# Front of a decoder step: squares of x in column strips, u in chunk order, all splits of x first, every low part on DVE

## Chip, cores and metric

One core of a Trainium2 chip runs one launch of the kernel. The metric is the time of that launch on the device in microseconds, median of several runs.

## What is computed

One inference step of a decoder layer, for a prompt of 512 tokens and eight samples of one token each. The kernel holds them together as T = 520 columns, with the 1024 features on the partitions (8 tiles of 128). The reference, cut to the part that the change touches:

```python
h = _rmsnorm(x, lp['g_mix'])                       # x * rsqrt(mean(x*x) + eps) * g
proj = h @ lp['w_in']                              # 1024 -> 2048
q, k, v, u = jnp.split(proj, [512, 1024, 1536], axis=-1)
...
lam_bar = jnp.exp(lam * dt)                        # S5: 32 groups, 64 complex states each
b_bar = ((lam_bar - 1.0) / lam)[..., None] * bmat
bu = jnp.einsum('gnp,btgp->btgn', b_bar, ug)
_, hs = lax.associative_scan(combine, (decay, bu), axis=1)     # h[t] = lam_bar*h[t-1] + bu[t]
y = jnp.einsum('gpn,btgn->btgp', cmat, hs).real + d_skip * ug
```

Behind it come stick-breaking attention over q, k, v (for the samples with paged keys and values), a gated output of the state-space part, the output projection, cross-attention into 256 memory tokens, a gated MLP with a convolution, and a final norm.

## The kernel before

Five engines run instruction lists of their own and meet at semaphores. The order on each is written out by hand.

**Weights.** All weights pass as 126 blocks of 128x1024 floats. SP loads block n into one of four raw buffers, once the low part of block n-4 is there. ACT rounds it to `w_hi` (`high(n)`, L1292), and a second engine subtracts to get `w_lo` (`low(n)`): DVE for the blocks in `DVE_LOWS` (whole, L1656), POOL for the others (two halves, L589). Both buffers are double. `high(n)` waits until block n-2 has been multiplied.

**A projection** (`project`, L625 to L627) takes 8 tiles of x, two halves of 260 columns, and three matmuls each (hi*hi, hi*lo, lo*hi): 48 matmuls. Blocks 0 to 3 give u, 4 to 7 q, 8 to 11 k, 12 to 15 v. Results stand in two alternating PSUM slots; DVE reads them, times the inverse root of the mean square `rinv` (`read_inputs`, L1769; `project_read`, L1809 and L1812), and a block waits for the read of the one two before it.

**Start.** ACT takes x in eight tiles: it rounds x*g to `h_hi` (L1311), DVE subtracts for `h_lo` (L1648), and ACT squares the tile into one of two buffers (L1325). TensorE multiplies block 0 tile by tile and after each tile adds the squares of that tile over the partitions, with a stationary of ones (128 wide, two matmuls of 260 columns in plain fp32, L707). ACT then takes the root (Ln, Exp, L1302 and L1303). Between the splits DVE computes powers of lambda on 128x16 operands.

**State-space part.** The prompt is cut into 128 chunks of 4 tokens. `turn_channels` (L719) brings u from (channel, time) into 32-row strips by position in the chunk: 64 matmuls with a slice of the identity, whose moving operand is every fourth column of u. `turn_weights` (L729) transposes the weights built by `lag_weights`, `lag_kernel` (L751) multiplies them with C, in 32 matmuls that fill 32-row strips, ACT copies the results (L1372, L1384). `chunk_states` (L770) gives the input of each chunk's state; DVE rotates it by the chunk's angle, scans over the chunks and rotates back (`rotate`, `scan`, `turn_back`, L1847 to L1873). The chunk angles are made on 128x2048 operands: ACT scales (L1347), DVE rounds off the whole turns (L1817 to L1819) and makes the absolute value (L1821), ACT takes two Sins (L1378, L1379). These steps lie between the projections of q and k. Then the first attention scores follow (L918), capped by DVE (L1933).

## Time and profile before

| | |
|---|---|
| median of 3 runs | 878.95 us (876.35 to 880.17) |
| profiled execution, own time | 880.04 us |
| its span | 878.3 us |
| TensorE matmul busy | 847.1 us (96%) |
| TensorE weight loads busy (beside the matmuls) | 797.1 us (91%) |
| DVE busy | 465.6 us (53%) |
| ACT busy | 334.0 us (38%) |
| POOL busy | 270.9 us (31%) |
| granted TensorE clock, mean | 0.991 of full |

Busy time is averaged over stages with different limits; in the first sixth of the span DVE is busy nearly all the time, later half of it. The page of the profile cuts the span in 40 slices of 22 us: DVE has 5, 9, 6, 9, 9, 8 tenths in the first six, TensorE 5, then 9 in nearly all. The chain that ended last is 84% TensorE.

### The profile page before, as it was taken

Reading aid. Unit: us, or ns where it says so; the run is one execution under the profiler, and the core shown is the slowest. Engines: PE = TensorE matmul, PEld = TensorE weight load, DVE = VectorE, ACT = ScalarE, POOL = GpSimd, SP = SyncE. Lnnn points to the kernel's source line nnn. Section 1 sums busy time; section 2 is a strip of 40 time slices with the busy share of each in tenths; the row PEclk is TensorE's granted clock in tenths of the full one; section 3 lists DMA queues with packets and bytes.
Section 4 is the critical chain, followed back from the end, with each engine's and each line's share of the span. In section 5 each row is a group of like instructions: output and inputs, shape, how many; then the busy total and the mean of one; then the engine's idle time right before and its main releaser. Section 6 shows DMA issues by size and latency. Waiting matters only on the chain.

```text
span 878.3 us, 17246 instructions
## 1 busy us (share of the span) xinstructions
PE 847.1 (96%) x7422; PEld 797.1 (91%) x7422; DVE 465.6 (53%) x674; ACT 334.0 (38%) x491; POOL 270.9 (31%) x213
## 2 busy tenths in 40 slices
PE   5999999999999999998999999999999999999996
PEld 4989998877888999995599999999999999999995
DVE  5969998777337735112323665656555666011013
ACT  6534415554745425113322633333333334222221
POOL 4100002010360151440025244444444444445560
PEclk9999999998999999999999999999999999999998
DMA  8211213233654485218412223322233322333312
GB/s 324 75 50 49 74 49 150 100 86 109 189 162 154 144 322 230 96 50 321 206 48 88 83 96 97 97 91 84 91 97 96 97 84 88 99 102 112 96 54 97
DMA packets 30459, 103.99 MB, mean 118 GB/s; under 512 B 3866, under 2 KB 6170, under 8 KB 27954
## 3 DMA queue, kind: packets, MB, share of 16 engines
q1 hardware_dynamic: 30386, 102.91, 34.8%
q8 instruction: 58, 0.95, 0.5%
q14 instruction: 15, 0.12, 0.0%
HBM read 96.28 MB, written 6.71 MB: 117 GB/s over the span
## 4 chain that ended last, share of the span: by engine, by line
PE 84%; DVE 5%; DMA 4%; ACT 4%; SPq 1%; issue 1%; POOL 0%; DVEq 0%; ACTq 0%
PE pj L625 22%; PE pj L627 22%; PE pj L626 22%; DMA w_raw<-in 3%; PE pj L1221 2%; PE aux L1152 2%; PE pj L632 2%; PE pj L634 1%; PE pj L633 1%; PE pj L918 1%; PE aux L707 1%; PE aux L719 1%; DVE near L1933 1%; PE aux L918 1%; ACT near L1424 1%
## 5 line engine op out<-in xcount | busy, mean ns | idle before, releaser
L589 POOL TENSOR_TENSOR w_lo<-w_raw,w_hi 128x512 fp32r<-128x512 f32 x196 | 260.6, 1350 | 553.9 <-ACT w_hi L1292 553.8
L625 PE MATMUL pj<-h_hi,w_hi 128*128 128x260 f32 x1312 | 374.4, 285 | 12.2 <-POOL w_lo L589 10.8
L627 PE MATMUL pj<-h_hi,w_lo 128*128 128x260 f32 x1312 | 371.3, 283 | 0.0
L626 PE MATMUL pj<-h_lo,w_hi 128*128 128x260 f32 x1312 | 370.1, 282 | 0.0
L625 PEld LDWEIGHTS pj<-h_hi,w_hi 128*128 128x128 f32 x1312 | 247.5, 189 | 14.1 <-POOL w_lo L589 10.8
L1292 ACT ACTIVATE w_hi<-w_raw 128x1024 fp32r<-128x1024 f32 x125 | 132.1, 1057 | 311.4 <-PE pj L627 274.0
L626 PEld LDWEIGHTS pj<-h_lo,w_hi 128*128 128x128 f32 x1312 | 247.3, 188 | 0.4
L627 PEld LDWEIGHTS pj<-h_hi,w_lo 128*128 128x128 f32 x1312 | 247.4, 189 | 0.0
L627 PE MATMUL pj<-a_hi,w_lo 128*128 128x260 f32 x336 | 95.0, 283 | 0.0
L625 PE MATMUL pj<-a_hi,w_hi 128*128 128x260 f32 x336 | 94.9, 282 | 0.0
L626 PE MATMUL pj<-a_lo,w_hi 128*128 128x260 f32 x336 | 94.9, 282 | 0.0
L627 PEld LDWEIGHTS pj<-a_hi,w_lo 128*128 128x128 f32 x336 | 63.3, 189 | 0.0
L625 PEld LDWEIGHTS pj<-a_hi,w_hi 128*128 128x128 f32 x336 | 63.2, 188 | 0.0
L626 PEld LDWEIGHTS pj<-a_lo,w_hi 128*128 128x128 f32 x336 | 63.2, 188 | 0.0
L2175 DVE TENSOR_TENSOR x<-pj,x 128x520 f32<-128x520 f32 x7 | 4.9, 700 | 88.4 <-PE pj L627 88.4
L2171 DVE TENSOR_TENSOR a_lo<-conv,a_hi 128x520 f32 x22 | 38.2, 1736 | 18.3 <-ACT a_hi L1614 18.3
L1644 DVE TENSOR_TENSOR acc<-acc,sq 128x520 f32<-128x520 f32 (+1 forms) x29 | 31.5, 1087 | 25.5 <-ACT sq L1298 25.5
L1611 ACT ACTIVATE conv<-conv 128x520 f32<-128x520 f32 x22 | 14.1, 639 | 74.6 <-DVE conv L2164 74.6
L1656 DVE TENSOR_TENSOR w_lo<-w_raw,w_hi 128x1024 fp32r<-128x1024 f32 x27 | 33.0, 1222 | 14.5 <-ACT w_hi L1292 14.3
L2160 DVE SCALAR_TENSOR_TENSOR conv<-gate,cols,conv 128x512 f32<-128x512 f32 x22 | 39.6, 1799 | 0.0
L2074 DVE TENSOR_TENSOR x<-pj,x 128x520 f32<-128x520 f32 x16 | 11.2, 699 | 35.4 <-PE pj L627 35.4
L2156 DVE TENSOR_TENSOR gate<-pj,rinv 128x520 f32<-128x520 f32 x22 | 15.4, 700 | 26.8 <-PE pj L627 26.5
(374 smaller groups left out, 1205.1 us busy)
## 6 DMA issues: line engine op xcount, KB each, us to landing
w_raw<-in SPq DMA_DIRECT2D x126, 512.0 KB, 3.5
caches<-in SPq DMA_DIRECT2D x14, 1024.0 KB, 12.3
vpg<-in SPq DMA_DIRECT2D x16, 256.0 KB, 2.9
kpg<-in SPq DMA_DIRECT2D x12, 256.0 KB, 3.0
x<-in SPq DMA_DIRECT2D x4, 520.0 KB, 8.4
out<-x SPq DMA_DIRECT2D x16, 130.0 KB, 1.9
out<-kT SPq DMA_DIRECT2D x1, 1040.0 KB
far<-in SPq DMA_DIRECT2D x1, 1024.0 KB, 4.8
```

The lines of the kernel that those rows point to most:

```text
L589: nc.gpsimd.tensor_tensor(lo[:, part], w_raw[:, n % 4, part], hi[:, part].bitcast(F32), ALU.subtract).then_inc(lo_done, 1)
L625: pe.matmul(out, s_hi, m_hi_, start=first, stop=False)
L626: pe.matmul(out, s_hi, m_lo_, start=False, stop=False)
L627: ins = pe.matmul(out, s_lo, m_hi_, start=False, stop=last)
L632: pe.matmul(out, stationary[0], moving[0], start=first, stop=False, skip_group_check=True)
L918: pe.matmul(at(h, i, P * i), kT[r0:r0 + DH, pair, P * i:P * (i + 1)], qT[r0:r0 + DH, pair, P * i:TP], start=(i < 3), stop=False, skip_grou ...
L1152: ins = pe.matmul(aux[:, 2 * (h % 2) + qt // 2, MT * (qt % 2):MT * (qt % 2 + 1)], qm[:, 2 * h + dd, P * qt:P * (qt + 1)], mkT[:, 2 * h + d ...
L1292: nc.scalar.activation(w_pair(n)[0], w_raw[:, n % 4, :], ACT.Copy).then_inc(hi_done, 1)
L1644: tt(acc[:, 0:width], acc[:, 0:width], sq[:, 0:width], ALU.add).then_inc(acc_added, 1)
L1656: tt(w_lo[:, n % 2, :], w_raw[:, n % 4, :], w_hi[:, n % 2, :].bitcast(F32), ALU.subtract).then_inc(dve_lo, 1)
L2160: order.done(stt(out=conv[:, c, 0:TP], in0=gate[:, c, 1:TP + 1], scalar=tap("conv_w1"), in1=conv[:, c, 0:TP], op0=ALU.mult, op1=ALU.add))
L2171: tt(a_lo[:, i * 2 + c, :], conv[:, c, :], a_hi[:, i * 2 + c, :].bitcast(F32), ALU.subtract).then_inc(a_split, 1)
```

## The change

- Squares: each of the eight tiles gets a buffer of its own (in tiles that are written later), so squares need no wait. TensorE sums them behind two tiles of block 1: four strips of 130 columns, each into 32 output rows, then ACT copies the strips to SBUF, and four matmuls with 32 contracted rows spread the sums to 128 rows (hence the factor GP in the mean).
- Splits: ACT rounds tiles 1 to 7 with only square 0, the angles and `high(1)` between; the other squares follow. DVE makes all low parts of x before the powers. SP loads x ahead of blocks 2 and 3 and the constants.
- Low parts 0, 1 and 2 go from POOL to DVE.
- u: `read_inputs` writes u by position in the chunk, so that `turn_channels` and the copies of the samples' u read it accordingly.
- Chunk angles: one rounding, and one fused operation (rounded minus ROUND minus angle, so the sign is turned); the absolute value goes to ACT.
- Order: `lag_kernel` goes ahead of the turned weights, its copy on ACT ahead of theirs; `input_products` and `input_weights` go behind the read of block 1 and low part 3; each of `read_inputs` 2 and 3 goes ahead of the lag weights beside it; `turn_back(0)` and low part 10 shift by one place; high(4) waits for the chunk numbers. POOL's two semaphores of the padding become one.

```diff
-DVE_LOWS = tuple(range(3, 16)) + tuple(range(N_MV, N_OUT + 2)) + (N_MQ, N_MQ + 1, N_GU, N_GU + 1)
+DVE_LOWS = tuple(range(16)) + tuple(range(N_MV, N_OUT + 2)) + (N_MQ, N_MQ + 1, N_GU, N_GU + 1)
...
+        def square_of_x(kt):
+            return (acc[:, :], sq[:, :], kT[:, 2, :], qT[:, 0, :], qT[:, 1, :], qT[:, 2, :], qT[:, 3, :],
+                    kT[:, 3, :])[kt]
+
+        QUARTER = T // 4
+
...
-            for c in range(4):
+            def load_x(c):
                 eng.dma_start(x[:, 2 * c:2 * c + 2, :], xT[:, 2 * c:2 * c + 2, :]).then_inc(x_loaded[c], 16)
-                load_block(c)
-                if c == 0:
-                    eng.dma_start(consts[:, :, :], consts_d).then_inc(consts_loaded, 16)
+
+            load_x(0)
+            load_block(0)
+            load_x(1)
+            load_block(1)
+            load_x(2)
+            load_x(3)
+            eng.dma_start(consts[:, :, :], consts_d).then_inc(consts_loaded, 16)
+            load_block(2)
+            load_block(3)
             eng.dma_start(bmat, bc_d[:, 0:2]).then_inc(s5_loaded, 16)
             eng.dma_start(cmat, bc_d[:, 2:4]).then_inc(s5_loaded, 16)
...
-            low(0)
-            low(1)
             pool.wait_ge(consts_loaded, 16)
             nc.gpsimd.tensor_copy(consts_r[:, :, :], consts[:, 0:3, :]).then_inc(consts_rounded, 1)
-            low(2)
-            pool.wait_ge(x_summed, KT)
+            pool.wait_ge(x_summed, 1)
             nc.gpsimd.memset(u_last, 0.0).then_inc(u_zeroed, 1)
             low(16)
             low(17)
             pool.wait_ge(y_done, 5)
...
                               halves(h_lo[:, kt, :])[:, a, :]) for a in range(2)], kt == 0, kt == KT - 1)
-                if kt == KT - 1:
-                    ins.then_inc(block_done, 1)
-                if kt == 0:
-                    pe.wait_ge(consts_loaded, 16)
-                pe.wait_ge(x_squared, kt + 1)
-                for a in range(2):
-                    ins = pe.matmul(aux[:, a, 0:HALF], ones, halves((sq, acc)[kt % 2][:, :])[:, a, :],
-                                    start=(kt == 0), stop=(kt == KT - 1))
+            ins.then_inc(block_done, 1)
+
+            def sum_squares():
+
+                pe.wait_ge(consts_loaded, 16)
+                for kt in range(KT):
+                    pe.wait_ge(x_squared, kt + 1)
+                    for s in range(4):
+                        ins = pe.matmul(aux[GP * s:GP * (s + 1), 3, 0:QUARTER], ones[:, 0:GP],
+                                        square_of_x(kt)[:, QUARTER * s:QUARTER * (s + 1)],
+                                        start=(kt == 0), stop=(kt == KT - 1), skip_group_check=True)
                 ins.then_inc(x_summed, 1)
+
+            def spread_sums():
+
+                pe.wait_ge(x_copied, 1)
+                for s in range(4):
+                    ins = pe.matmul(aux[:, s, 0:QUARTER], ones[GP * s:GP * (s + 1), :],
+                                    rinv[GP * s:GP * (s + 1), 0:QUARTER], start=True, stop=True,
+                                    skip_group_check=True)
+                ins.then_inc(x_summed, 1)
+
             def turn_channels():
 
                 pe.wait_ge(evacuated, 4)
...
-                        moving = uT[:, a, 0:TP].rearrange("p (c j) -> p j c", j=CH)
+                        moving = uT[:, a, :].rearrange("p (j c) -> p j c", j=CH)[:, :, 0:NCH]
...
             def turn_weights(g):
                 b, wt = g // 2, (wtre, wtim)[g % 2]
+                if g == 2:
+                    pe.wait_ge(kernel_copied, 1)
+                if g == 3:
+                    pe.wait_ge(rc_copied, 1)
                 if g >= 4:
                     pe.wait_ge(w2_copied, g - 1)
                 for r in range(4):
...
             def lag_kernel():
 
-                pe.wait_ge(w2_copied, 8)
+                pe.wait_ge(wt_built, 1)
...
             def turn_kernel():
 
-                pe.wait_ge(kernel_copied, 1)
+                pe.wait_ge(w2_copied, 8)
...
 
-            for n in range(1, N_Q + 1):
+            ready(1, 1)
+            for kt in range(KT):
+                if kt == 2:
+                    sum_squares()
+                if kt == KT // 2:
+                    second_half(1)
+                if kt == KT // 2:
+                    spread_sums()
+                hi, lo = weight(1, kt)
+                ins = three([(slot(1)[:, a, :], hi, lo, halves(h_hi[:, kt, :])[:, a, :],
+                              halves(h_lo[:, kt, :])[:, a, :]) for a in range(2)], kt == 0, kt == KT - 1)
+            ins.then_inc(block_done, 1)
+            for n in range(2, N_Q + 1):
                 project(n, n)
             turn_channels()
             project(N_Q + 1, N_Q + 1)
             column_scales()
-            pe.wait_ge(wt_built, 1)
-            for g in range(3):
+            lag_kernel()
+            for g in range(4):
                 turn_weights(g)
-            pe.wait_ge(rc_copied, 1)
-            turn_weights(3)
             project(N_Q + 2, N_Q + 2)
             chunk_states(0)
             for g in range(4, 8):
...
             def square_x(kt):
-                if kt >= 2:
-                    act.wait_ge(x_summed, kt - 1)
-                nc.scalar.activation((sq, acc)[kt % 2][:, :], x[:, kt, :], ACT.Square).then_inc(x_squared, 1)
-
-            for kt in range(KT):
+                nc.scalar.activation(square_of_x(kt), x[:, kt, :], ACT.Square).then_inc(x_squared, 1)
+
+            def split_x(kt):
                 act.wait_ge(x_loaded[kt // 2], 16)
                 split_high(kt, "g_mix")
-                if kt == 0:
-                    high(0)
-                if kt == 2:
-                    high(1)
+
+            split_x(0)
+            high(0)
+            split_x(1)
+            square_x(0)
+            act.wait_ge(angle_done, 1)
+            nc.scalar.activation(sm[:, 11, :], sm[:, 9, :], ACT.Exp)
+            nc.scalar.activation(sm[:, 14:16, :], sm[:, 12:14, :], ACT.Sin).then_inc(polar_done, 1)
+            split_x(2)
+            split_x(3)
+            high(1)
+            for kt in range(4, KT):
+                split_x(kt)
+            for kt in range(1, KT):
                 square_x(kt)
-                if kt == 1:
-                    act.wait_ge(angle_done, 1)
-                    nc.scalar.activation(sm[:, 11, :], sm[:, 9, :], ACT.Exp)
-                    nc.scalar.activation(sm[:, 14:16, :], sm[:, 12:14, :], ACT.Sin).then_inc(polar_done, 1)
+            nc.scalar.preload_act_table_set("natural_log_exp_and_others")
+            act.wait_ge(x_summed, 1)
+            nc.scalar.activation(rinv[:, 0:QUARTER], aux[:, 3, 0:QUARTER], ACT.Copy).then_inc(x_copied, 1)
             high(2)
-            act.wait_ge(x_summed, KT)
-            nc.scalar.preload_act_table_set("natural_log_exp_and_others")
-            inverse_root(halves(rinv[:, :]), sums01, D)
+            act.wait_ge(x_summed, 2)
+            inverse_root(rinv[:, :].rearrange("p (s t) -> p s t", s=4), aux[:, :, 0:QUARTER], GP * D)
             high(3)
+            act.wait_ge(turns_ready, 1)
             high(4)
-            act.wait_ge(turns_ready, 1)
             for k in range(PAIRS):
                 ins = nc.scalar.activation(eim[:, k, :], chunk_no, ACT.Copy, scale=sm[:, 33, k:k + 1])
...
-                        uT[rows, :, TP:T], ACT.Copy)
+                        edge[GP * lane:GP * (lane + 1), :, :].rearrange("p (a q) b -> p a q b", q=4)[
+                            :, :, q, 0:NS].rearrange("p a (c j) -> p a c j", j=CH),
+                        uT[rows, :, :].rearrange("p a (j c) -> p a c j", j=CH)[:, :, NCH:T // CH], ACT.Copy)
             ins.then_inc(u2_act, 1)
...
 
+            act.wait_ge(kernel_done, 1)
+            nc.scalar.activation(kernel_cols, aux[:, 2, :], ACT.Copy).then_inc(kernel_copied, 1)
             for g in range(4):
                 copy_weights(g)
             act.wait_ge(e_angle, 1)
-            nc.scalar.activation(eim, eim, ACT.Sin, scale=2.0 * PI_IN)
+            order.done(nc.scalar.activation(ere, eim, ACT.Abs))
+            nc.scalar.activation(eim, eim, ACT.Sin, scale=-2.0 * PI_IN)
             nc.scalar.activation(ere, ere, ACT.Sin, scale=-2.0 * PI_IN, bias=HALF_PI).then_inc(e_done, 1)
             high(8)
             for g in range(4, 8):
                 copy_weights(g)
-            act.wait_ge(kernel_done, 1)
-            nc.scalar.activation(kernel_cols, aux[:, 2, :], ACT.Copy).then_inc(kernel_copied, 1)
             high(9)
             act.wait_ge(k0_added, 1)
...
 
-            between = (powers, angle_2, angle_4, power_2, power_3)
             for kt in range(KT):
                 split_low(kt, "g_mix", kt + 1)
-                if 2 <= kt < 7:
-                    between[kt - 2]()
+                if kt == 0:
+                    low(0)
+            low(1)
+            powers()
+            angle_2()
+            angle_4()
+            power_2()
+            power_3()
             last_power()
             input_gain()
+            low(2)
 
...
             t4 = [tmp[:, i, :].rearrange("p (k g) -> p k g", k=PAIRS) for i in range(4)]
-            dve.wait_ge(s5_loaded, 32)
-            tt(t4[0], bmat[:, 0], wide(16), ALU.mult)
-            tt(t4[1], bmat[:, 1], wide(32), ALU.mult)
-            tt(t4[2], bmat[:, 0], wide(32), ALU.mult)
-            order.done(tt(t4[3], bmat[:, 1], wide(31), ALU.mult))
+
+            def input_products():
+                dve.wait_ge(s5_loaded, 32)
+                tt(t4[0], bmat[:, 0], wide(16), ALU.mult)
+                tt(t4[1], bmat[:, 1], wide(32), ALU.mult)
+                tt(t4[2], bmat[:, 0], wide(32), ALU.mult)
+                order.done(tt(t4[3], bmat[:, 1], wide(31), ALU.mult))
+
+            def input_weights():
+                tt(wtre[:, :, 3, :], t4[0], t4[1], ALU.add)
+                order.done(tt(wtim[:, :, 3, :], t4[2], t4[3], ALU.add))
 
             def read_inputs(a):
                 dve.wait_ge(block_done, a + 1)
-                tt(halves(uT[:, a, :]), slot(a), halves(rinv[:, :]), ALU.mult).then_inc(evacuated, 1)
+                tt(uT[:, a, :].rearrange("p (j a c) -> p a j c", j=CH, a=2),
+                   slot(a).rearrange("p a (c j) -> p a j c", j=CH),
+                   rinv[:, :].rearrange("p (a c j) -> p a j c", a=2, j=CH), ALU.mult).then_inc(evacuated, 1)
 
             def lag_weights(a):
                 cmul(wtre[:, :, 2 - a, :], wtim[:, :, 2 - a, :], wtre[:, :, 3, :], wtim[:, :, 3, :],
...
             read_inputs(0)
-            tt(wtre[:, :, 3, :], t4[0], t4[1], ALU.add)
-            order.done(tt(wtim[:, :, 3, :], t4[2], t4[3], ALU.add))
             chunk_turns()
             nc.vector.tensor_tensor_scan(chunk_no, ones, ones, -1.0, ALU.mult, ALU.add).then_inc(turns_ready, 1)
             read_inputs(1)
             low(3)
+            input_products()
+            input_weights()
+            read_inputs(2)
+            low(4)
             lag_weights(0)
-            low(4)
-            read_inputs(2)
+            read_inputs(3)
+            low(5)
             lag_weights(1)
-            low(5)
-            read_inputs(3)
+            low(6)
             lag_weights(2)
-            low(6)
 
 
             def project_read(n):
...
             order.done(ts(ere, eim, ROUND, None, ALU.add))
-            order.done(ts(ere, ere, ROUND, None, ALU.subtract))
-            order.done(tt(eim, eim, ere, ALU.subtract))
+            stt(out=eim, in0=ere, scalar=ROUND, in1=eim, op0=ALU.subtract, op1=ALU.subtract).then_inc(e_angle, 1)
+            project_read(N_Q + 1)
             low(7)
-            stt(out=ere, in0=eim, scalar=-1.0, in1=eim, op0=ALU.mult, op1=ALU.max).then_inc(e_angle, 1)
-            project_read(N_Q + 1)
             output_gain(0)
             project_read(N_Q + 2)
...
 
-            dve.wait_ge(u2_act, 2)
             output_gain(1)
             low(8)
             rotate(0)
             scan(0)
-            turn_back(0)
             project_read(N_Q + 3)
             low(9)
             add_skip()
+            turn_back(0)
+            dve.wait_ge(u2_act, 2)
             project_read(N_K)
             rotate(1)
+            low(10)
             scan(1)
-            low(10)
             project_read(N_K + 1)
             low(11)
             turn_back(1)
```

## Rows read from the trace of the kernel before

**Rows 1.** Stretches of the front: length, busy us per engine, granted clock, DMA share, GB/s.

```profile
11.00:16.20 5.20, 5.20 (x19) 4.67 (x20) 3.11 (x9) 4.46 (x8) 3.33 (x3) 1.00 1.02 416
16.20:26.15 9.95, 9.95 (x64) 9.21 (x63) 8.99 (x45) 6.44 (x10) 1.62 (x2) 1.00 0.58 187
26.15:31.90 5.75, 5.75 (x51) 5.75 (x50) 5.71 (x6) 2.81 (x4) 3.56 (x3) 1.00 0.22 63
31.90:49.10 17.20, 17.20 (x148) 17.06 (x151) 16.89 (x29) 7.87 (x19) 0.00 (x0) 1.00 0.29 101
49.10:56.60 7.50, 7.50 (x130) 4.64 (x129) 7.36 (x8) 2.86 (x4) 0.00 (x0) 1.00 0.24 76
56.60:138.50 81.90, 80.67 (x771) 77.86 (x771) 72.78 (x125) 28.31 (x43) 0.00 (x0) 1.00 0.15 46
```

**Rows 2.** Waits of TensorE, first 150 us: total us, times, longest.

```profile
PE pj L625 <- POOL w_lo L589: 10.8, 1, 10.8
PE aux L751 <- ACT near L1372: 0.7, 1, 0.7
PE pj L625 <- DVE w_lo L1656: 0.3, 1, 0.3
```

**Rows 3.** Timeline of TensorE at its start: start us, us, instruction.

```profile
11.60 0.42 PE L625 MATMUL pj<-h_hi,w_hi 128*128 128x260 f32 x1
11.81 0.42 PE L626 MATMUL pj<-h_lo,w_hi 128*128 128x260 f32 x1
```

**Rows 4.** Chain of waits, 10 to 80 us: start us, us on it, engine and line.

```profile
12.45 1.73 PE aux L707 x4
...
17.30 0.88 PE aux L707 x4
...
49.11 7.49 PE aux L719 x120
56.60 0.32 PE pj L625
...
75.85 1.96 PE aux L751 x64
```

**Rows 5.** Timeline of ACT.

```profile
8.32 1.06 ACT L1292 ACTIVATE w_hi<-w_raw 128x1024 fp32r<-128x1024 f32 x1 [2.36 <-DMA w_raw<-in]
9.28 0.62 ACT L1325 ACTIVATE sq<-x 128x520 f32<-128x520 f32 x1
9.81 0.71 ACT L1311 ACTIVATE h_hi<-x,cols 128x520 fp32r<-128x520 f32 x1
...
11.16 1.28 ACT L1338 ACT_TABLE_LOAD   x1
...
28.38 0.64 ACT L1303 ACTIVATE rinv<-rinv 128x520 f32<-128x520 f32 x1
...
69.27 1.89 ACT L1379 ACTIVATE keys<-keys 128x2048 f32<-128x2048 f32 x1
```

**Rows 6.** Timeline of DVE; in brackets idle time before, and what ended it.

```profile
15.73 1.72 DVE L1648 SCALAR_TENSOR_TENSOR h_lo<-x,cols,h_hi 128x520 fp32r<-128x520 f32 x1
...
28.39 1.77 DVE L1764 TENSOR_TENSOR vtok<-u,sm 128x512 f32<-128x512 f32 x1
...
34.49 1.22 DVE L1656 TENSOR_TENSOR w_lo<-w_raw,w_hi 128x1024 fp32r<-128x1024 f32 x1
...
53.69 1.23 DVE L1818 TENSOR_SCALAR keys<-keys 128x2048 f32<-128x2048 f32 x1
54.95 2.29 DVE L1819 TENSOR_TENSOR eim<-eim,keys 128x2048 f32<-128x2048 f32 x1
63.79 1.23 DVE L1656 TENSOR_TENSOR w_lo<-w_raw,w_hi 128x1024 fp32r<-128x1024 f32 x1 [6.55 <-ACT w_hi L1292]
...
71.85 0.70 DVE L1809 SCALAR_TENSOR_TENSOR qT<-pj,rinv 128x520 f32<-128x520 f32 x1
...
141.60 1.68 DVE L1933 TENSOR_SCALAR near<-aux,cap 128x1024 f32<-128x1024 f32 x2 [2.52 <-PE aux L922]
```

More of the change, by code:

```diff
@@ L255, in build @@
         x_summed = sem("x_summed")
+        x_copied = sem("x_copied")
         e_angle = sem("e_angle")
@@ L312, in build @@
         o_read = sem("o_read")
-        qdz_ready = sem("qdz_ready")
+        pads_ready = sem("pads_ready")
         masks_ready = sem("masks_ready")
@@ L777, in sample_states @@
                     pe.wait_ge(u2_act, 2)
-                    pe.wait_ge(kernel_copied, 1)
+                    pe.wait_ge(w2_copied, 8)
                 else:
@@ L1006, in decode_pages @@
                     pe.wait_ge(y_read, AT)
[L1007 removed]
+                    pe.wait_ge(pads_ready, 2)
                 for n in range(first, last):
```

10 lines of the change are left out of this document (3 added, 7 removed).

## Prediction

> **What bounds the kernel now.** I read the table of stretches first [rows 1]. Its column PE busy equals the length of each stretch up to 56.60 us, and from 56.60 to 138.50 only 1.23 of 81.90 us are idle: TensorE is the bound. The list of TensorE's waits [rows 2] then holds 10.8 us for the first low part and three short waits (0.7, 0.2 and 0.3 us; the rows of 0.7 and 0.3 are shown). So time comes out of this front only through matmul time taken away, through the first start, or through those short waits. DVE is close behind: busy 16.89 of 17.20 and 72.78 of 81.90 us. Whether a saving on TensorE arrives has to be checked against DVE's queue, where [rows 6] show the room: 6.55 us idle before the low part at 63.79, and 2.52 us before it caps the first scores at 141.60.
>
> **The change part by part.** "Tile" below is one kt of a projection: six matmuls of 260 columns. In the block from 26.15 to 31.90, eight tiles took 5.75 us, 0.72 each [rows 1]. Up to about 16.2 us the same matmuls start 0.21 to 0.22 us apart instead of 0.12 [rows 3], so a tile takes 1.3 us there; these fit the clock's two levels (1.2 and 2.4 GHz), although the column of granted clock shows 1.00 throughout. I keep the rise at 16.2.
>
> *Sums of squares.* Before: two matmuls of 260 columns, 128 wide, per tile. The chain of waits gives them 1.73 us at the start, then 1.10 and six times 0.88 (the first and one of the six are shown [rows 4]): 8.1 us. After: 32 matmuls of 130 columns that each fill a strip of 32 output rows, then four that spread the sums. The nearest row is the lag kernel, 32 matmuls of 128 columns into the same kind of strips: 1.96 us [rows 4]. A 128-wide one of 260 columns takes 0.44, so of 130 columns 0.22; 32 of them one after the other would be 7.0 us. The lag kernel has this very form, so I take 2.0, and keep 7.0 as the other end. The spread has four matmuls with 32 contracted rows: 0.88 in turn, 0.22 if they overlap. No row shows such row strips, I take 0.88.
> The end of a strip group has a price in the trace: the first matmul after the channel turn takes 0.32 on the chain against 0.12 [rows 4], 0.2 us. Two groups inside block 1 add 0.4.
> The Trainium skill, "TensorEngine Tiling (Array Packing)", Key Properties, says that changing the tiling mode drains TensorE; that speaks against two small groups in the middle of a block, and the 0.2 us just named is what this trace shows of it. If each entry cost the same again, it would be 0.4 us more.
>
> *When block 1 ends.* Low part 0 moves from POOL to DVE; both can start when ACT has rounded w_hi at 9.4 [rows 5]; DVE takes 1.22 for the whole [rows 6], and POOL's first half released TensorE at 10.8 [rows 2]. I take 10.7 as the start. Tiles 0 and 1: to 13.3. ACT meanwhile does split 1, square 0, an Exp, the table load of 1.28, the Sin and split 2; it ends that at 12.8 instead of 13.3, since one square is gone in front (square and split start 0.53 and 0.62 apart, the load takes 1.28 [rows 5]). DVE adds 0.7, tile 2 starts at 13.5; tiles 2, 3 slow and 4 to 7 fast: 13.5 + 2.6 + 2.9 = 19.0. The splits follow each other every 0.6 to 0.7 us and stay ahead (the last low part of x at 17.9). Then DVE does low part 1, 1.2 us: 19.1. Two tiles: 20.5. ACT's seven squares (0.53 apart, after the last split at 16.9) end at 20.7; sums to 22.6; two tiles 24.0; spread 24.9; four tiles 27.8; the two transitions 28.2. Ahead of the spread ACT loads its table (20.7 to 22.0) and copies the strips by 22.9, in time. Block 2 started at 31.90. **Gain 3.7 us.**
> Does DVE allow block 2 at 28.2? Behind low part 1 it does the small powers and gains, that before lay between the splits: about 5.9 us of short operations, to 25.0. Low part 2 to 26.2 (ACT rounds w_hi 2 behind the copy, by 24.0), and the first read of u, which waits for the root (Ln and Exp, 0.6 each [rows 5]: 26.2), to 26.9. A margin of 1.3 us.
>
> *Channel turn.* 64 matmuls of 128 columns, 7.49 us; the lag kernel's 32 take 1.96, so 64 would be 3.9 [rows 4]. Both write four strips in turn. What differs is the moving operand: the turn reads every fourth element of u, the lag kernel reads contiguously. With u in chunk order the turn reads contiguously. Ends: 7.49 (the cause is another) and 3.9. I take 3.9: **gain 3.6 us.**
> The Trainium skill, "SBUF — State Buffer", section "Door 1: The DMA port swizzle", gives a cause: lines of 16 bytes, with a penalty for each access to a new line. The old turn meets a new line at every element, which agrees with the factor 1.9 between the rows. The rule cuts the other way for the new reads of u, which step by 16 bytes through rinv and PSUM. By the same factor they would cost DVE 4 x 0.6 us more.
>
> *DVE.* Three low parts come to it: +3.5 us. POOL's go, and with them slow stretches beside them: a split of 1.72 us, a 128x512 product of 1.77 against 0.69 [rows 6], five such places (1.0, 1.0, 0.3, 1.1, 1.1), -4.5. Chunk angles: the second ROUND (1.23 [rows 6]) and the absolute value (2.3, as the subtraction of 2.29 beside it [rows 6]) go, and the subtraction becomes one fused operation of the same width: -3.5. New reads of u: between nothing and +2.5 as above, by ordinary rows nothing. All this lies ahead of the 6.55 us of idle time at 63.79, which absorbs it. The low parts 3 to 6 must only be there before their blocks: each is at least 4 us early.
> ACT gets a 2048-wide Abs of about 1.8 us (its Sin of the same width takes 1.89 [rows 5]) and a small copy; u's 16 angle scalings start a high part later. Abs lies in front of rounding w_hi 8 and of copies 4 to 7 of the turned weights, where TensorE waits 0.7 and 0.2 already. Worked through, copy 4 is ready about 0.9 us after TensorE wants it, as before: nothing. A table load of its own for Abs would add 1.3; the other end.
>
> *The lag kernel moves ahead* of the turned weights. It waits for the third lag weights on DVE (about 51 us, while TensorE comes at 56). The fourth group of turned weights waits for copies behind it, covered by the two that come first. Neutral. It puts the end of block 6 at 71.1 - 7.3 + 2.0 = 65.8.
>
> *From block 6 to the scores.* DVE reads block 6 at 71.85 and has 67.2 us until it stands still at 139.1, with 1.3 idle in it (low(12) 0.6, block 9 0.5, 0.2), some 66.5 now. TensorE has 70.5 from the end of block 6 to the end of the first scores, now less 2.0 and less the wait of 0.3 [rows 2]: 68.2. So DVE is ready 1.7 us before it is needed, where it was 2.5. **Gain 0.3 us** from the wait. SP: x goes ahead of w 2, w 3 and the constants; x's last tile is then some 0.8 MB earlier in the queue, at the 416 GB/s of 11.0 to 16.2 [rows 1] 1.9 us. The constants are first needed at 20.5, w 2 at 22.9. Low part 1 comes at 19.1 instead of 16.9, so w 5 lands later, but it is rounded only at 39. Nothing.
>
> *Behind.* From 138.5 on everything hangs on events of this chain (page loads on y, weights on low parts, caches on the output projection), nothing on absolute time. The shift is kept.
>
> Sum: 3.7 + 3.6 + 0.3 = 7.6 us of the profiled execution's 880.04: 872.4. That execution lies 1.1 above the median of three, so 878.95 - 7.6 = **871.3**.
>
> **The rivals.**
> B, the stride isn't what slows the channel turn (it may be the identity as stationary, or the alternation of four slices). For: only one row with a stride. Against: all other strip groups run at twice its rate. 871.3 + 3.6 = 874.9.
> C, the change doesn't do what it says: the strips of sums don't overlap. 32 x 0.22 = 7.0 in place of 2.0: 876.3. Against it the lag kernel, the same form.
> D, DVE becomes the bound between block 6 and the scores. For: it works there almost without a pause, and has 1.7 us left. If its part grows by 4.5 us (waiting for ACT's late cosines, late low parts), 2.8 us are lost: 874.1.
> E, slower: the clock. The first two blocks are now fed by ACT's splits and squares; if TensorE's small waits (tile 2, block 1, the squares) keep the low level past 16.2, each block runs at 0.215 instead of 0.12 us per matmul, 10.3 instead of 5.75: 4.6 us. It decides from 1.7 blocks on; three blocks give 871.3 + 13.8 = 885.1. Against: TensorE waited as long before 16.2 in the old order and the pace rose.
>
> **How the numbers follow.** Forecast 0.70 (own range 868.3 to 873.3: down for an overlapping spread 0.7, free transitions 0.4, earlier first weights 0.7 and 1.2 of scatter; up for a table load before Abs 1.3 and 0.7 of small waits), B 0.10, D 0.11, C 0.04, E 0.05. What a measurement here tells from nothing is 0.5%, 4.4 us: faster means below 874.6. All of the forecast's range and most of D are there, B at its edge: faster 0.82, same 0.14, slower 0.04. Range for 8 in 10: 867.8 to 875.0, which takes in B and D.
>
> **What would show it.** Right: four strip sums of about 2 us inside block 1, block 2 starting near 28, the channel turn at 3.9 us in about 45 to 49, the read of block 6 near 66, the first capping near 134. Wrong: matmuls 0.22 us apart after 17 us (E), a turn of 7.5 us (B), sums of 7 us (C), TensorE waiting for low parts or reads between 66 and 134 (D). The whole prediction is wrong if the shift at the first capping is there and the end doesn't show it.

## Result and the profile after

The changed kernel took 869.57 us (868.84 to 871.08, five runs) against 878.01 (876.35 to 880.17, five runs) on the same chip: ratio 0.991, 95% interval 0.989 to 0.993, so 8.4 us faster. The forecast was 7.6 us, to 871.3. The kernel before had 878.95 in its first three runs; 878.01 is the median of these and two more. Its profiled execution took 868.84 us, its span is 867.0.

The page of the changed kernel, its head:

```profile
span 867.0 us, 17322 instructions
## 1 busy us (share of the span) xinstructions
PE 835.3 (96%) x7462; PEld 788.4 (91%) x7462; DVE 463.0 (53%) x675; ACT 335.0 (39%) x493; POOL 262.8 (30%) x207
```

TensorE's busy time fell by 11.8 us, the span by 11.3, and the share stayed 96%: work was taken off the engine that sets the end. The stretches of the changed kernel, cut at the first matmul, the end of block 0, the end of block 1, the start and the end of the channel turn, and the end of v's third block. The columns are those of [rows 1], whose table starts 0.2 us behind the first matmul (10.78) and cuts block 0 once more, at 16.20:

```profile
10.17:18.44 8.27, 8.04 (x48) 7.35 (x48) 6.01 (x10) 8.26 (x14) 0.51 (x1) 1.00 1.05 389
18.44:27.20 8.76, 8.76 (x123) 8.15 (x123) 8.10 (x50) 5.32 (x8) 0.53 (x1) 1.00 0.37 123
27.20:44.41 17.21, 17.21 (x148) 17.07 (x151) 17.01 (x24) 7.84 (x19) 0.00 (x0) 1.00 0.32 112
44.41:48.05 3.64, 3.64 (x130) 3.44 (x129) 3.57 (x6) 2.78 (x4) 0.00 (x0) 1.00 0.15 39
48.05:128.80 80.75, 80.08 (x771) 77.73 (x771) 75.61 (x130) 30.08 (x44) 0.00 (x0) 1.00 0.16 53
```

Blocks 2 to 4 take 17.2 us before and after. The gain lies on either side of them: the turn is reached 4.7 us earlier (0.6 of it by an earlier first matmul) and is 3.9 shorter, and the stretch behind it is 80.75 instead of 81.90. The chain of waits of the changed kernel from 12 to 66 us answers to [rows 4]. Here L719 is the strip sums, L728 the spread, L742 the turn:

```profile
20.14 1.91 PE aux L719 x64
22.05 0.32 PE pj L635
23.69 0.43 PE aux L728 x8
24.12 0.32 PE pj L635
44.41 3.63 PE aux L742 x128
48.05 0.32 PE pj L635
```

Each group is followed by one matmul of 0.32 us instead of 0.12, as behind the old turn. DVE in the changed kernel, the rows that answer to [rows 6]: a read of u, the fused angles, the read of block 6, the first capping:

```profile
33.76 1.10 DVE L1825 TENSOR_TENSOR kT<-pj,rinv 128x520 f32<-128x520 f32 x1
...
52.64 2.29 DVE L1876 SCALAR_TENSOR_TENSOR eim<-keys,eim 128x2048 f32<-128x2048 f32 x1
...
64.47 0.70 DVE L1867 SCALAR_TENSOR_TENSOR qT<-pj,rinv 128x520 f32<-128x520 f32 x1 [3.81 <-PE pj L637]
...
131.89 1.68 DVE L1989 TENSOR_SCALAR near<-aux,cap 128x1024 f32<-128x1024 f32 x2 [1.67 <-PE aux L958]
```

The first capping of scores starts at 131.89 instead of 141.60, 9.7 us earlier, and DVE still waits 1.67 us for it.

**A better ruler.** The runs above differ by 2.2 us for the changed kernel and by 3.8 for the one before (later, by up to 6.2), more than most of the questions below ask for. The front can be read far more sharply: from the first matmul to the first capping. That is 130.82 us before and 121.72 after, so 9.1. The other 0.6 of the 9.7 lie ahead of the first matmul. Most of it (0.5) is the landing of the first weights: ACT starts to round block 0 at 8.32 us before and at 7.80 after. This puts the first matmul anywhere from 9.6 to 10.8 us in the profiles of all kernels here. From now on "front" means this distance, and "turn" the distance from the first matmul to the channel turn (38.26 before, 34.17 after). The ruler has a scatter of its own: three profiles of the changed kernel have fronts of 121.11, 121.72 and 121.96 us, so a front between 121.1 and 122.0 can't be told from the changed kernel's.

### The profile page after: what moved, and what is told of

The parts are those of the page before. It is cut to its first block, busy times and chain, and to the rows that moved or that the text cites. A ratio compares the mean times of both kernels' runs of the same rounds, so it can differ in the third digit from the quotient of the medians.

```text
span 867.0 us, 17322 instructions
## 1 busy us (share of the span) xinstructions
PE 835.3 (96%) x7462; PEld 788.4 (91%) x7462; DVE 463.0 (53%) x675; ACT 335.0 (39%) x493; POOL 262.8 (30%) x207
## 4 chain that ended last, share of the span: by engine, by line
PE 83%; DVE 6%; ACT 5%; DMA 4%; issue 1%; SPq 1%; DVEq 0%; ACTq 0%
PE pj L635 22%; PE pj L637 22%; PE pj L636 22%; DMA w_raw<-in 3%; PE pj L1257 2%; PE aux L1188 2%; PE pj L642 1%; PE pj L644 1%; PE pj L643 1%; DVE near L1989 1%; DMA caches<-in 1%; PE pj L954 1%; PE aux L954 1%; ACT near L1468 1%; ACT near L1469 1%
## 5 line engine op out<-in xcount | busy, mean ns | idle before, releaser
L602 POOL TENSOR_TENSOR w_lo<-w_raw,w_hi 128x512 fp32r<-128x512 f32 x190 | 252.8, 1352 | 533.1 <-ACT w_hi L1328 533.0
L1700 DVE TENSOR_TENSOR w_lo<-w_raw,w_hi 128x1024 fp32r<-128x1024 f32 x30 | 36.6, 1221 | 7.3 <-ACT w_hi L1328 7.0
```

What stands on the lines that cost most here:

```text
L602: nc.gpsimd.tensor_tensor(lo[:, part], w_raw[:, n % 4, part], hi[:, part].bitcast(F32), ALU.subtract).then_inc(lo_done, 1)
L1700: tt(w_lo[:, n % 2, :], w_raw[:, n % 4, :], w_hi[:, n % 2, :].bitcast(F32), ALU.subtract).then_inc(dve_lo, 1)
```

## Experiments

**The changed kernel again**, no edit, beside the next three kernels.

> The changed kernel once more, as the base of this call. Theory (the gain is made in the front, 9.7 us at the first capping of scores, and kept): 869 to 871 us against 877 to 879 before, block 2 starts at about 27.2 us, the channel turn takes 3.6 us, the first capping starts at 131.9 us. Rival (the front's gain is partly given back later, since the medians differ by only 8.4 us): first capping as stated, but the end under 8 us ahead of before when both have the same granted clock between 200 and 280 us.

870.92 us against 878.05 (ratio 0.9926, 0.9905 to 0.9947). Front 121.96, turn 3.6 us, DVE's room 1.67. From the first capping to the end of the span it took 736.7 us, as the kernel before (878.3 - 141.60 = 736.7), the first changed profile 735.1. The end lies 9.8 us ahead of the kernel before, not under 8; but the rival asked for equal clocks between 200 and 280 us, and they are not equal (the kernel before has two falls there, this profile none). So nothing behind the front is gained, and the question whether something is given back stays open until the section "Behind the front". What differed most in the front was when the matmul pace rose. The timeline of TensorE in this run:

```profile
15.35 0.42 PE L637 MATMUL pj<-h_hi,w_lo 128*128 128x260 f32 x1
15.56 0.36 PE L635 MATMUL pj<-h_hi,w_hi 128*128 128x260 f32 x1
15.76 0.28 PE L636 MATMUL pj<-h_lo,w_hi 128*128 128x260 f32 x1
15.88 0.28 PE L637 MATMUL pj<-h_hi,w_lo 128*128 128x260 f32 x1
```

and in a later run of the very same kernel (the last but one below):

```profile
12.40 0.38 PE L635 MATMUL pj<-h_hi,w_hi 128*128 128x260 f32 x1
12.62 0.29 PE L636 MATMUL pj<-h_lo,w_hi 128*128 128x260 f32 x1
12.74 0.28 PE L637 MATMUL pj<-h_hi,w_lo 128*128 128x260 f32 x1
```

Starts 0.22 us apart become 0.12 apart at 15.8 and at 12.6 us; in the first profile of the changed kernel it was 13.7.

**u back in time order**

```diff
-                tt(uT[:, a, :].rearrange("p (j a c) -> p a j c", j=CH, a=2), ...
+                tt(halves(uT[:, a, :]), slot(a), halves(rinv[:, :]), ALU.mult)
...
-                        moving = uT[:, a, :].rearrange("p (j c) -> p j c", j=CH)[:, :, 0:NCH]
+                        moving = uT[:, a, 0:TP].rearrange("p (c j) -> p j c", j=CH)
...
```

(The copies of the samples' u on ACT read u accordingly.)

> The changed kernel with u back in time order (reads, channel turn and the copies of the samples' u as before). Theory (the step of 16 bytes of the moving operand halves the rate): the channel turn takes 7.5 us again instead of 3.6, the four reads of u on DVE 0.69 us instead of 1.09, everything behind is 3.8 us later, first capping at 135.7 us, total 873 to 874.5. Rival (the turn became faster for another reason, such as the copies or the tiles it shares banks with): the turn stays below 4.5 us and the total within 0.5 us of the changed kernel.

The chain of this kernel has, where the changed one has 3.63:

```profile
44.22 7.49 PE aux L742 x119
```

and its reads of u take 0.70 us on DVE instead of 1.10. Front 125.60: 3.6 to 3.9 us more than the two changed profiles so far. The theory held on the trace. The rival is out, since the turn was not below 4.5 us. What was put back is the order of u, so also the four reads and eight small copies of the samples' u on ACT; but TensorE waits for none of them, and the copies start at 52.26, when the turn is over. The moving operand is what is left. The total was 876.38 (ratio 0.9977, 0.9959 to 0.9994), above the expected 873 to 874.5 and 5.5 above the changed kernel beside it, where the front says 3.6. Its one profile shows 2.8 us more in one stretch behind the front (see "Behind the front"); whether that accounts for the median of ten runs is not shown.

**The sums 128 rows wide again, at the new place**

```diff
-                    for s in range(4):
-                        ins = pe.matmul(aux[GP * s:GP * (s + 1), 3, 0:QUARTER], ones[:, 0:GP], ...
+                    for a in range(2):
+                        ins = pe.matmul(aux[:, a, 0:HALF], ones, halves(square_of_x(kt))[:, a, :], ...
...
-                    spread_sums()
...
```

(ACT's copy of the strips goes too, and it takes the root straight from the sums.)

> The changed kernel with the sums of squares 128 rows wide again (16 matmuls of 260 columns at the same place in block 1, no copy and no spread). Theory (column strips save TensorE time, and TensorE sets the end): the sums take 7.0 us instead of 1.9 + 0.4 and one 0.2 us transition, block 2 starts 4.5 us later, first capping at 136.4, total 873.5 to 875. Rival (what counts was to take the squares out of the wait between ACT and TensorE in block 0; the strips only free time that TensorE then waits for DVE): block 2 under 2 us later, total within 1.5 us of the changed kernel.

Its chain:

```profile
20.07 7.01 PE aux L719 x32
```

7.01 against 1.91 + 0.43 us. Turn 38.47, front 126.01: 4.1 to 4.3 us more than in the changed kernel, nearly all of its gain ahead of the turn (4.1). So it is the strips that saved the time: with wide sums, all that the change does ahead of the turn, taking the squares out of block 0 among it, saved nothing (38.47 against 38.26). Total 873.69 (ratio 0.9951, 0.9934 to 0.9969), as expected, 2.8 above the changed kernel where the front says 4.1.

**Low parts 0 to 2 back on POOL**

```diff
-DVE_LOWS = tuple(range(16)) + ...
+DVE_LOWS = tuple(range(3, 16)) + ...
...
```

(The three low parts move from DVE's list to POOL's, to their places in the kernel before.)

> The changed kernel with low parts 0 to 2 back on POOL. Theory (low parts of the first three blocks are hidden wherever they are made): TensorE starts within 0.3 us of 10.2, block 2 within 0.5 us of its start in the changed kernel, total within 0.5 us. Rival (POOL beside DVE slows both; with the squares out of the way low part 2 comes last): low part 2 finishes after 26 us and DVE's short operations and its first read of u end 1 to 3 us later, so block 2 starts 1 to 3 us later and the total grows by as much.

Front 123.06, 1.1 to 1.3 more than in the two changed profiles so far (1.9 more than in the later one, with 121.11). The total was 872.01 (ratio 0.9928, 0.9908 to 0.9949) against 870.92, which is within the noise. The size is the rival's, the place is another: low part 2 does end late, at 27.8 us, but TensorE doesn't wait for it. DVE's last four splits of x, and TensorE's waits, in this kernel:

```profile
14.93 4.56 DVE L1695 SCALAR_TENSOR_TENSOR h_lo<-x,cols,h_hi 128x520 fp32r<-128x520 f32 x4 [0.76 <-ACT h_hi L1350]
```

```profile
PE pj L638 <- POOL w_lo L602: 10.7, 1, 10.7
PE pj L638 <- DVE h_lo L1695: 1.5, 2, 0.8
```

The four splits take 2.77 us in the changed kernel, 4.56 beside POOL's low part 1 (14.36 to 17.35), and TensorE waits 1.5 us for two of them, instead of 0.2.

**The kernel before with chunk order alone** (the second experiment's edit, the other way, on the kernel before)

> The kernel before with u in chunk order alone (reads, channel turn, copies of the samples' u). Theory (the gain of the turn is independent of the rest and passes to the end): turn 3.6 us instead of 7.5, first capping at 137.7 us instead of 141.6 if DVE can follow, total 874 to 875. Rival (DVE, which had 2.5 us of room before the first capping, becomes the bound: its three low parts fewer don't help, and the four reads cost it 1.6 us): first capping at 138.5 us or later with DVE not waiting for TensorE there, total above 875.5.

Front 126.93 against 130.82: 3.9 us, the turn 3.63, and DVE's wait before the first capping is 2.53 as before. The reads' extra 1.6 us vanish in DVE's idle time. Total 874.0 (871.98 to 876.47) against 877.38: ratio 0.9966 (0.9952 to 0.9980). The parts of the gain add: 3.9 for the turn here, 4.3 for the strips (from the wide sums), 1.2 for the low parts, together 9.4 against 9.1.

**22 multiplications of zeros ahead of block 0**

```diff
+            pe.wait_ge(u_zeroed, 1)
+            zeros = u_first[:, :, :].rearrange("p k b -> p (k b)")
+            for _ in range(22):
+                pe.matmul(aux[:, 0, 0:P], zeros, zeros, start=True, stop=True)
             ready(0, 0)
```

> The changed kernel with 22 plain fp32 multiplications of zeros ahead of block 0 (they add to the work; their result is not used). Theory (block 0 is bound by ACT's and DVE's splits of x, so the low clock of its first 3.3 us costs little): if the clock is up when block 0 starts, block 0 ends at most 0.3 us earlier, since low part 7 of x ends at 17.2 and low part 1 at 18.4; total within 0.5 us. Rival (the clock costs what its matmuls are longer): about 15 matmuls 0.1 us shorter, block 1 starts 1.5 us earlier, total 1.5 us less.

The zeros run from 1.0 to 8.8 us, and block 0 starts at the high pace. But its waits:

```profile
PE pj L635 <- DVE w_lo L1704: 1.9, 1, 1.9
PE pj L635 <- DVE h_lo L1696: 1.7, 2, 1.2
```

The first row is the wait ahead of block 0. In block 0 TensorE now waits 1.7 us for splits of x. Turn 34.17, front 121.71, as in the changed kernel; total 871.6 (867.64 to 873.85). The theory held: the time won by the pace is lost again in waits for the splits.

**The late Sin**

```diff
-            split_x(1)
-            square_x(0)
+            for kt in range(1, 4):
+                split_x(kt)
+            high(1)
+            for kt in range(4, KT):
+                split_x(kt)
             act.wait_ge(angle_done, 1)
...
-                if kt == 2:
+                if kt == KT // 2:
                     sum_squares()
...
-                if kt == KT // 2:
+                if kt == KT // 2 + 1:
                     spread_sums()
```

> The changed kernel with the Exp, the Sin and its table load, and square 0, behind all splits of x, and with the strip sums behind four tiles of block 1 and the spread behind five. Theory (the splits set block 0 and low part 1): splits end 2.1 us earlier, block 1 starts at about 17.2 instead of 18.4, block 2 at 25.9 instead of 27.2, all behind 1.3 us earlier, total 869 to 870 where the changed kernel has 870.5. Rival (DVE's powers then come too late: low part 2 and the read of block 0 set block 2): block 2 waits for the read and starts within 0.4 us of 27.2, total unchanged.

Front 121.40, 0.3 less, which the scatter of the ruler doesn't tell from nothing; total 871.42 (869.82 to 873.84), not the expected 869 to 870. TensorE waits for no split, but 0.3 us for the read of block 0, as the rival had it, and block 2 starts at 26.67 instead of 27.2. So of the 1.3 us expected 0.5 came. The pace was low until 14.0 us; that TensorE itself was now the slower part in block 0 is what the next kernel tests.

**Both**

> Both of the two kernels above. Theory: with the splits out of the way the clock counts, block 1 starts at 16.2 us and block 2 at 24.9, so 2.3 us less than the changed kernel, total 868 to 869. Rival (multiplying zeros doesn't raise the clock, or DVE's read of block 0 sets block 2): the same as with the late Sin alone, or less than 0.5 us better.

Front 120.68, 0.4 to 1.3 less than the three profiles of the changed kernel, 0.7 less than with the late Sin alone; block 2 starts at 25.63, 24.9 was expected. Total 867.27 us (866.81 to 868.22), ratio 0.9892 (0.9865 to 0.9919), less than the expected 868 to 869, though only 1.0 of the expected 2.3 us came in the front. The wait for the read of block 0 (0.3) is there as in the kernel above.

**Chunk angles on DVE as before**

```diff
-            stt(out=eim, in0=ere, scalar=ROUND, in1=eim, op0=ALU.subtract, op1=ALU.subtract)
+            order.done(ts(ere, ere, ROUND, None, ALU.subtract))
+            order.done(tt(eim, eim, ere, ALU.subtract))
+            stt(out=ere, in0=eim, scalar=-1.0, in1=eim, op0=ALU.mult, op1=ALU.max)
```

> The changed kernel with the chunk angles made as before (second rounding, subtraction and absolute value on DVE, no Abs on ACT). Theory (DVE has idle time there: 3.8 us before it reads block 6, so the 3.5 us moved off it were hidden): first capping 121.7 us after the first matmul as in the changed kernel, within 0.3; DVE's wait before block 6 falls from 3.8 to about 0.3 us; ACT gets past its Sins 2 us sooner, so the 0.7 us wait of the turned weights goes, first capping at most 0.7 us earlier. Rival (the shorter angles were part of the gain: DVE is short of time there): first capping 1 to 3 us later than in the changed kernel.

The read of block 6 in this kernel:

```profile
64.37 0.70 DVE L1866 SCALAR_TENSOR_TENSOR qT<-pj,rinv 128x520 f32<-128x520 f32 x1 [0.20 <-PE pj L637]
```

The idle time of 3.81 us is filled and nothing is late. TensorE's wait for the copied weights is 0.3 instead of 0.7. Front 121.28, within the scatter of the ruler; total 870.19, one run. The new angles gave nothing, and by that wait they cost 0.4 us.

**The loads in the old order**

```diff
             load_block(0)
+            eng.dma_start(consts[:, :, :], consts_d).then_inc(consts_loaded, 16)
             load_x(1)
             load_block(1)
             load_x(2)
+            load_block(2)
             load_x(3)
-            eng.dma_start(consts[:, :, :], consts_d).then_inc(consts_loaded, 16)
-            load_block(2)
             load_block(3)
```

> The changed kernel with SP's loads in the order of before (constants behind block 0, blocks 2 and 3 between the x). Theory (the order was hidden or worth a few tenths): first matmul between 9.6 and 10.8 us as in all runs so far; h_lo of the last tiles waits for x: before, the last x landed at about 15.4 us where its split is now wanted at 14.3, so block 0 ends up to 1.5 us later and the first capping lies 121.7 to 123.2 us after the first matmul. Rival (landing is early enough in either order): 121.7 within 0.2 us.

Behind the first tile nothing waits for x in the trace. The front is 122.12, with a pace that rose at 16.5 us. The changed kernel has 121.11, 121.72 and 121.96 with rises at 12.6, 13.7 and 15.8, so the late rise can account for the difference. By its number the theory's range holds and the rival's 0.2 us doesn't; by the missing wait the rival is right. The total is 870.86 us, one run. One profile can say no more.

**The changed kernel and the one with both, side by side**

> The changed kernel beside the next one on the same chip: 869.5 to 871.5 us; first capping 121.7 to 122.0 us after the first matmul.

869.69 us (868.51 to 871.86) against 876.20, ratio 0.992 (0.9901 to 0.994). The front was 121.11, below the expected range, with the earliest rise of the pace.

> The changed kernel with the late Sin and the 22 multiplications of zeros, again, with more rounds. Theory (1.0 us of the front, all that its trace showed, is what it is worth; the 3.6 us between the medians were scatter behind the front): 868.5 to 870.5 us, 0.5 to 1.5 us below the changed kernel of this call. Rival (the early multiplications also change something behind the front): again 3 us or more below it.

868.12 us (865.34 to 869.76), ratio 0.990 (0.9879 to 0.9921): 1.6 us below the changed kernel, the size that the theory had. The intervals overlap, so that it beats the changed kernel is likely, not shown. And the theory's reason is not borne out: the front was 121.22, no better than the 121.11 beside it. So the 1.0 us of the front did not repeat, and what difference there is between these two profiles lies behind the front. The timeline of TensorE shows what happened to the front:

```profile
10.21 0.39 PE L635 MATMUL pj<-h_hi,w_hi 128*128 128x260 f32 x1 [2.35 <-DVE w_lo L1701]
10.43 0.28 PE L636 MATMUL pj<-h_lo,w_hi 128*128 128x260 f32 x1
...
11.39 0.42 PE L635 MATMUL pj<-h_hi,w_hi 128*128 128x260 f32 x1
11.61 0.42 PE L636 MATMUL pj<-h_lo,w_hi 128*128 128x260 f32 x1
...
14.83 0.28 PE L636 MATMUL pj<-h_lo,w_hi 128*128 128x260 f32 x1
```

After 2.35 us of waiting the pace was still high, fell at 11.4 and came back at 14.8. In the two other kernels with zeros the wait was 1.9 and 1.6 us, and the pace stayed high.

## Why the prediction was right, by its steps

- *The whole.* The number was met (8.4 against 7.6), and the mechanism of each of its two large terms was shown. That the number is this close is in part luck: in the front the gain was larger than forecast (9.1 us from the first matmul to the first capping, 9.7 at the capping itself), and behind the front some of it is missing again.
- *TensorE is the bound.* Right: busy time and span fell together.
- *Sums of squares.* 2.0 us for the strips, measured 1.91; 7.0 for wide ones, measured 7.01. The spread was mis-sized: 0.88 forecast, 0.43 measured, half of four in turn. This fits matmuls on separate groups of 32 contracted rows that overlap in part; no row shows one of them alone. Two transitions at 0.2: right. A second price for entering a group is not visible: 64 strips take 3.63 us and the lag kernel's 32 take 1.86 in the changed kernel, which by an estimate from these two leaves 0.1 us that doesn't grow with their number. The Trainium skill says in "TensorEngine Tiling (Array Packing)", Key Properties, that changing the tiling mode drains TensorE; this trace shows 0.2 us behind a group for it, and at most that 0.1 ahead of one.
- *When block 1 ends.* 28.2 forecast, 27.2 measured: 0.5 of it because the first matmul came at 10.17 and not at 10.7, the other 0.5 by the spread. "I keep the rise at 16.2" is the term that doesn't hold as a constant: the pace rose between 12.6 and 16.5 us over the kernels without zeros. In the first changed profile the early rise (13.7) gave little, since TensorE then waited for a split (0.2 us) and could begin block 1 only with low part 1, at 18.4: block 0 took 8.27 us, 8.4 was forecast. From the first matmul to the turn the gain forecast was 3.6 (3.7 less the 0.1 by which the first matmul was to come earlier). The three profiles of the changed kernel give 38.26 less 34.44, 34.17 and 33.57: 3.8 to 4.7, more the earlier the pace rose.
- *Low parts to DVE: costed at no gain.* Wrong: 1.1 to 1.9 us of the front, by which of the three changed profiles one takes. I gave DVE's shorter operations to its idle time at 63.79, but four of them are splits of x, and once the squares no longer stand between the tiles, TensorE waits for these (1.5 us instead of 0.2).
- *Channel turn.* 3.6 forecast, 3.86 measured. The stride was the cause, shown from both sides: put back it costs the 3.86 again, and alone in the kernel before it gives them.
- *Reads of u.* I took 0.69 us, measured 1.10. The Trainium skill ("SBUF — State Buffer", "Door 1: The DMA port swizzle") states a penalty for each access to a new line of 16 bytes. The trace agrees that there is one: a factor of 1.6 here, where the turn has 2.1. These reads step by 16 bytes in PSUM and in SBUF at once; which of the two costs the time is not shown. The 1.6 us of the four reads were hidden in DVE's idle time.
- *DVE's room before the scores.* 1.7 forecast, 1.67 measured, and this is luck: two errors cancel. The forecast's 66.5 us for DVE don't follow from its own terms (67.2 less 1.3 is 65.9), and DVE took 65.75 (64.47 to 130.22). The 68.2 us for TensorE were 67.5 (the end of block 6, at 64.4, to 131.89). The 3.8 us idle in front of block 6 is what is left of 6.55.
- *Angles and Abs.* Neutral forecast; the Abs costs 0.4 us through the copies it delays. The Abs brought no table load of its own, so the forecast's other end (1.3 us) did not occur: the timeline has one load between Abs and Sin, as before between copies and Sin.
- *From the turn to the capping.* 0.3 forecast; measured 141.60 - 56.60 less 131.89 - 48.05, 1.2. The timelines place it. The two pauses of the projections on either side of block 6 (transposed weights, lag kernel, first chunk states), from the last projection matmul ahead to the first behind, are 2.84 and 6.91 us before, 4.62 and 4.51 after: 0.6 less, of which a wait of TensorE for copied weights is 0.2. The pause behind the third group of chunk states, where the 0.3 us wait for a low part was, is 2.37 before and 1.83 after: 0.5 less. All other pauses are equal. "Neutral" for moving the lag kernel was thus a little too low.
- *Behind: "the shift is kept".* Only in part. The fronts differ by 9.1; the medians of the three sets of runs by 8.4, 7.1 and 6.5. What the profiles show of the difference is in the next section.
- *The rivals.* B: the turn takes 3.63 us and not 7.5. C: the strips take 1.91 and not 7.0. D: DVE has its 1.67 us of room. E: no matmuls 0.22 us apart after 17 us. So none of them occurred. The argument against E was misread, though: TensorE did not wait "as long before 16.2 in the old order", since [rows 1] has it busy for 5.20 of 5.20 us up to there. What speaks against E is only seen now: the pace rose in each of the changed kernel's profiles, in the first one at 13.7 us.

## Behind the front

From the first capping to the end of the span the fourteen profiles took 733.7 to 739.7 us, in no order of their fronts. Two things carry this. The first is a wait. Around 390 to 410 us TensorE waits twice for the cached memory keys, here in the kernel before and then in the changed one:

```profile
PE pj L1171 <- DMA caches<-in: 2.0, 2, 1.4
PE pj L1207 <- DMA caches<-in: 3.4, 2, 2.8
```

The changed kernel has 3.4, 3.2 and 3.5 us in its three profiles, so it gives back 1.2 to 1.5 us here. The kernel before, chunk order alone, wide sums and both profiles of the best kernel have 2.0 to 2.4, the kernel with zeros alone 2.9, all others 3.4 to 3.6. This also is a part of what puts the wide sums nearer to the changed kernel than their front says, and the best kernel below it with the same front. In all of them the loads are issued 4.7 to 5.7 us before the first of the two waits ends; why the data of the second land later in some is not known.

The second is the clock. In three places the column of granted clock falls in some executions. For the kernel before, two of the places:

```profile
196.00:214.00 18.00, 16.48 (x140) 13.35 (x130) 13.92 (x21) 8.12 (x12) 0.00 (x0) 0.81 0.49 147
262.00:274.00 12.00, 10.88 (x78) 9.93 (x71) 6.70 (x10) 4.78 (x6) 0.95 (x1) 0.86 0.59 198
```

For the changed kernel's last profile, the first place again and the third, beside the waits for the cached memory keys:

```profile
194.00:206.00 12.00, 11.31 (x56) 8.62 (x60) 9.58 (x14) 5.97 (x10) 0.00 (x0) 0.72 0.42 126
391.00:400.00 9.00, 6.22 (x41) 4.54 (x34) 0.94 (x3) 1.16 (x3) 0.00 (x0) 0.81 1.00 413
```

The falls order the profiles. From the first capping to the end, those without a fall took 733.7 and 734.3 us, those with the first alone 734.4 to 735.1, those with the third alone 736.6 to 737.0, and those with two of the three 736.7 to 739.7. The second place was seen in two profiles, the kernel before and u in time order. Both take 57.2 and 57.4 us from the last values' load to the store of the memory keys, all others 54.6 to 55.7; it is the 2.8 us above. In front of it TensorE had waited 1.1 and 1.4 us for DVE's write of the mask `az`; in the others this wait is 0 to 1.2 us. The third separates the profiles cleanly: the six without a fall there (before, the first changed one, wide sums, chunk order alone, both profiles of the best) take 530.2 to 532.0 us from the store of the memory keys to that of the gates, the eight with one 533.5 to 535.2. The 532.0 are those of the first changed profile, which has the long wait without the fall; so the wait alone costs about 1 us and the fall at least 1.5 more. At each of the three places TensorE waits, but it waits there in executions without a fall too.

The changed kernel has the third fall in two of its three profiles and the kernel before in none of its one. The mean clock that each run leaves points the same way: 0.998, the value of the one profile that has no fall at all (chunk order alone), stands in 11 of the 44 later runs of the kernel before and in none of the 15 runs of the changed kernel. So the longer wait for the cached keys and a more frequent fall there can explain medians 0.7 to 2.6 us short of the front's 9.1. The wait is shown in the profiles; that the change causes either is not, and what decides whether a given wait brings a fall stays open.

## To carry to other kernels

In a kernel whose TensorE is busy all the way, look at the matmuls that are not the projections. The sum of one tile's squares with a stationary of ones took 0.88 us, more than the six projection matmuls of a tile (0.72), and 32-row strips made the eight sums a quarter (7.0 to 1.9 us, 2.3 with the spread). A moving operand in steps of 16 bytes doubled the turn (3.6 to 7.5). Write the operand in the order in which TensorE will read it, even if the writer gets slower, as long as the writer has idle time afterwards. Measure between two events of the trace rather than by the total when the scatter of the total is as large as the question, and then look behind the second event as well: a gain that arrives there can be lost in part at a later wait.

## What the runs showed of the hardware

- The pace of the first matmuls doubled 3.0 to 6.1 us after the first of them, at different times with the same instructions (3.0, 3.5 and 5.9 in three profiles of the changed kernel), while the column of granted clock read 1.00. The column does show the fall in the best kernel's last profile: 0.73 from 10 to 13 us and 0.70 from 13 to 16.
- Plain fp32 matmuls of zeros brought the high level (block 0 then began at 0.12 us spacing in all three profiles with them). In one of them, after a wait of 2.35 us, it was lost for 3.4 us, although TensorE had been working again for 1.2 us when it fell.
- With POOL subtracting beside DVE, four splits of x on DVE took 4.56 instead of 2.77 us, 1.14 instead of 0.69 each on average.
- A DVE multiplication of 128x520 elements took 0.70 us contiguous and 1.10 with steps of 16 bytes in PSUM and SBUF.
- 32 fp32 matmuls of 130 columns into strips of 32 rows took 1.91 us, 16 of 260 columns into 128 rows 7.01, and the first matmul behind a group of strips 0.32 instead of 0.12.
